# Weight-block sums of a two-level block-product FFN: from instructions on GpSimd to accumulating transfers

## The reference

```
def conv_ffn(hn, w_ffn_in, conv_w, conv_b, w_ffn_down):
    u, v = jnp.split(hn @ w_ffn_in, 2, axis=-1)          # 1024 -> 2 x 2816
    uc = conv_b
    for t in range(CONV_W):                               # width 3
        uc = uc + up[:, t:t + L] * conv_w[t]
    return (jax.nn.gelu(uc) * v).astype(dt) @ w_ffn_down  # 2816 -> 1024
```

## Time and profile before

| | us |
|---|---|
| median of 3 runs | 1282.95 (1281.03 to 1283.58) |
| the profiled execution | 1282.7 |
| its span, first to last instruction | 1280.9 |
| TensorE busy | 1219.8 (95%) |
| VectorE busy | 875.3 (68%) |
| ACT busy | 528.7 (41%) |
| GpSimd busy | 195.6 (15%) |

### The profile page before, as it was taken

One profiled execution on the slowest core, in us unless ns is written; L12 is line 12 of the kernel. 1 busy time (PEld: TensorE's weight loads), 2 busy tenths in 40 slices (PEclk: granted clock), 3 DMA queues, 4 the chain that ended last, 5 costly groups with the idle time before them and its releaser, 6 DMA issues.

```text
span 1280.9 us, 18435 instructions
## 1 busy us (share of the span) xinstructions
PE 1219.8 (95%) x6989; PEld 1108.8 (87%) x6989; DVE 875.3 (68%) x1189; ACT 528.7 (41%) x832; POOL 195.6 (15%) x137
## 2 busy tenths in 40 slices
PE   6999999999999999999999979899899899899977
PEld 5999999999999988888888869789789789789965
DVE  7494585486377372232233799988998998898987
ACT  5353353335245152122221456535535535535544
POOL 0000000000000000000000314324324333433340
PEclk9999999999999999999999999999899899899989
DMA  4311111101201011111123012112121121121302
GB/s 168 134 35 49 68 44 50 61 33 49 78 33 49 34 54 62 66 62 69 65 94 131 22 66 80 53 68 81 50 77 72 50 83 66 50 82 67 115 17 99
DMA packets 23185, 86.14 MB, mean 67 GB/s; under 512 B 2512, under 2 KB 2768, under 8 KB 23120
## 3 DMA queue, kind: packets, MB, share of 16 engines
q1 hardware_dynamic: 22544, 83.90, 17.7%
q10 hardware_dynamic: 576, 1.38, 0.3%
HBM read 82.12 MB, written 3.15 MB: 67 GB/s over the span
## 4 chain that ended last, share of the span: by engine, by line
PE 83%; DVE 10%; issue 2%; DVEq 2%; ACT 1%; DMA 1%; POOL 0%; SPq 0%; ACTq 0%; POOLq 0%
PE ps L1507 43%; PE ps L1750 19%; PE ps L1833 10%; PE ps L1604 3%; PE ps L1544 3%; DVE ring L1232 2%; PE ps L1597 1%; PE ps L1614 1%; PE ps L1532 1%; DVE cb L1315 1%; DVE cb L1296 1%; DVEq L1301 1%; DVE af L1251 1%; PE ps L1534 1%; DVE h L1219 1%
## 5 line engine op out<-in xcount | busy, mean ns | idle before, releaser
L1507 PE MATMUL ps<-hn,ring 128*128 128x256 f32 (+1 forms) x2544 | 462.6, 337 | 0.3 <-DVE hn L921 0.3
L1507 PEld LDWEIGHTS ps<-hn,ring 128*128 128x128 f32 x2544 | 388.3, 191 | 46.7 <-issue 0.7
L1750 PE MATMUL ps<-af,ring 128*128 128x384 f32 x1848 | 334.0, 340 | 33.0 <-DVE v L1288 21.0
L1750 PEld LDWEIGHTS ps<-af,ring 128*128 128x128 f32 x1848 | 325.8, 191 | 40.3 <-DVE v L1288 22.3
L1833 PE MATMUL ps<-ring,gf 128*128 128x512 f32 x693 | 161.0, 394 | 7.1 <-DVE gf L1331 6.8
L892 DVE TENSOR_TENSOR ring<-raw,ring 128x1024 fp32r<-128x1024 f32 x68 | 83.1, 1224 | 119.2 <-ACT ring L476 114.8
L1833 PEld LDWEIGHTS ps<-ring,gf 128*128 128x128 f32 x693 | 132.0, 191 | 35.1 <-issue 7.8
L1232 DVE TENSOR_TENSOR ring<-raw,ring 128x512 fp32r<-128x512 f32 x164 | 127.5, 810 | 13.5 <-ACT ring L713 13.3
L713 ACT ACTIVATE ring<-raw 128x512 fp32r<-128x512 f32 x164 | 96.6, 621 | 53.2 <-DMA raw<-in_pairs 42.0
L1467 POOL TENSOR_TENSOR sums<-raw 128x512 f32<-128x512 f32 x1 | 1.3, 1283 | 707.0 <-DMA raw<-in_pairs 707.0
L525 ACT ACTIVATE sig<-ps 128x768 f32<-128x768 f32 x36 | 29.2, 812 | 179.9 <-PE ps L1507 179.9
(11 more groups left out here) (171 smaller groups left out, 1297.8 us busy)
## 6 DMA issues: line engine op xcount, KB each, us to landing
raw<-in_units SPq DMA_DIRECT2D x68, 512.0 KB, 3.4
raw<-in_pairs SPq DMA_DIRECT2D x66, 512.0 KB, 3.5
strips<-in_strips SPq DMA_DIRECT2D x4, 896.0 KB, 4.6
x_in<-in_x_s SPq DMA_DIRECT2D x4, 512.0 KB, 5.4
h<-in_x_s SPq DMA_DIRECT2D x1, 2048.0 KB, 8.0
y_s<-hw SPq DMA_DIRECT2D x4, 512.0 KB, 3.0
x_in<-in_x_p SPq DMA_DIRECT2D x2, 512.0 KB, 7.4
h<-in_x_p SPq DMA_DIRECT2D x1, 1024.0 KB, 10.4
```

Of the source, the lines that this page charges most:

```text
L1507: ins = pe.matmul(out, w if stationary_w else x, x if stationary_w else w, start=start and i == 0, stop=stop and i == 2)
L1750: ins = pe.matmul(ps[:, bank, 0:HALF], ring[:, p, a, k * P:(k + 1) * P], af[:, x, b, k, :], start=first and k == 0 and j == 0, stop=k == H ...
```

## The change

All sums of weight blocks become additions, so that a transfer can make them: S1 = b11+b12, S3 = b12+b22, S2 = b11+b12+b22, A22 = S2+b21. The token forms, joins, gate sums and residuals change their signs to suit (S2's and S3's results are subtracted from the residual).

- The sums of pairs 1 and on are made by transfers that add a block from HBM to what lies in SBUF (`accum_op=ALU.add`). GpSimd issues them, in the order S2, S3, S1, A22. S2 has three addends: SP loads b11 a second time from HBM into the pair's "second" buffer, a transfer adds b12, GpSimd waits for its semaphore `half_sum`, and another adds b22. So S2 doesn't wait for S1. A22 adds b21 to S2, once S2 is split.
- SP's first load of a pair now waits for A12 and S1 of the buffer's pair before, the new 256 KB load for its A22, the second load for its S3 and S4. Pair 0's sums stay instructions on GpSimd; pair 1's three leave VectorE.
- Order on VectorE: the four gate sums are a function of their own, `gate_sums`, which comes behind `join_third` of the next pair. At a stage's end `conv`, `gate` and `gate_lo` of its last pair each come one down form later. In the last stage `gate_lo(20)` comes ahead of the convolution, and two forms of pair 21 ahead of the gate sums. ACT's gelu moves to suit.
- At the start of the feed-forward part TensorE takes S1 of pair 0 ahead of its S2, and VectorE and ACT make the token forms in that order.

```diff
+        def sum_weights(pool, j, x):
+            b = raw_of(j)
+            r, second = raws[b], seconds[b]
+            u, v = pairs[j, 0], pairs[j, 1]
+            if x == S3:
+                pool.wait_ge(pv_ld[b], 16 * loads_of(j))
+                out, block = r[:, 1, 0:PIECE], v[:, PIECE:UNIT]
             elif x == S2:
+                pool.wait_ge(sec_ld[b], 16 * sums_of(j))
+                pool.dma_start(second, v[:, 0:PIECE], accum_op=ALU.add).then_inc(half_sum[b], 16)
+                pool.wait_ge(half_sum[b], 16 * sums_of(j))
+                out, block = second, v[:, PIECE:UNIT]
+            elif x == S1:
+                pool.wait_ge(pu_ld[b], 16 * loads_of(j))
+                pool.wait_ge(flo, ORD[j, A11] + 1)
+                out, block = r[:, 0, 0:PIECE], v[:, 0:PIECE]
             else:
+                pool.wait_ge(flo, ORD[j, S2] + 1)
+                out, block = second, u[:, PIECE:UNIT]
+            pool.dma_start(out, block, accum_op=ALU.add).then_inc(t_sum[x][b], 16)
...
                 else:
-                    sp.wait_ge(flo, ORD[prior, A22] + 1)
+                    sp.wait_ge(flo, max(ORD[prior, A12], ORD[prior, S1]) + 1)
                 sp.dma_start(raws[b][:, 0, :], pairs[j, 0]).then_inc(pu_ld[b], 16)
+                if j > 0:
+                    if prior is not None:
+                        sp.wait_ge(flo, ORD[prior, A22] + 1)
+                    sp.dma_start(seconds[b], pairs[j, 0][:, 0:PIECE]).then_inc(sec_ld[b], 16)
                 if prior is not None:
-                    sp.wait_ge(flo, ORD[prior, S4] + 1)
+                    sp.wait_ge(flo, max(ORD[prior, S3], ORD[prior, S4]) + 1)
                 sp.dma_start(raws[b][:, 1, :], pairs[j, 1]).then_inc(pv_ld[b], 16)
...
                     if i > 0:
                         join_third(i)
+                    if i > lo and i % 2 == 0:
+                        gate_sums(i - 1)
                     if i > lo and i < NF - 1:
                         gate_lo(i - 1)
                 lo_upto(PLACE[hi - 1, A22] + 5)
                 lo_upto(PLACE[hi - 1, S4] + 5)
                 join_last(hi - 1)
-                conv(hi - 1)
                 if hi == NF:
+                    gate_lo(NF - 2)
+                    conv(hi - 1)
                     gate(NF - 1)
-                    gate_lo(NF - 1)
+                    gate_lo(NF - 1, GATES[1:3])
+                    gate_sums(NF - 1)
+                    gate_lo(NF - 1, GATES[3:])
                 for n, x in enumerate(DOWN[d]):
...
                         if n == 0:
+                            conv(hi - 1)
+                        elif n == 1:
                             gate(hi - 1)
-                        elif n == 1:
+                        elif n == 2:
                             gate_lo(hi - 1)
...
             pool.wait_ge(y_done, NT + 2)
             for x in SUMS:
                 combine_tokens(pool, 0, x, s_done, 0)
 
-            pool.wait_ge(t_done, DIFF[1, S3])
-            for j, x in DIFFS[7:]:
-                difference(pool, j, x)
+            for j, x in SUMMED[4:]:
+                sum_weights(pool, j, x)
```

More of the change, by code:

```diff
@@ L78, in taken @@
         if i == 0:
-            out += [(0, A11), (0, A12), (1, A11), (1, A12), (0, S2), (0, S1), (0, S3)]
+            out += [(0, A11), (0, A12), (1, A11), (1, A12), (0, S1), (0, S2), (0, S3)]
             continue
@@ L111 @@
     SEQ += list(range(_lo, _hi)) + [down_pair(_q) for _q in _qs]
-    DIFFS += [(_i, _x) for _i in range(_lo, _hi) for _x in (S1, S2, S3, A22)]
-    DIFFS += [(down_pair(_q), _x) for _xs in ((S1, S2), (S3,), (A22,)) for _q in _qs for _x in _xs]
-DIFF = {_f: _n + 1 for _n, _f in enumerate(DIFFS)}
+    SUMMED += [(_i, _x) for _i in range(_lo, _hi) for _x in (S2, S3, S1, A22)]
+    SUMMED += [(down_pair(_q), _x) for _xs in ((S2, S3), (S1,), (A22,)) for _q in _qs for _x in _xs]
 LAST_Q = NQ - 1
@@ L124, in loads_of, with sums_of @@
     return sum(raw_of(i) == raw_of(j) for i in SEQ[:SEQ.index(j) + 1])
+def sums_of(j):
+    return sum(i > 0 and raw_of(i) == raw_of(j) for i in SEQ[:SEQ.index(j) + 1])
 def prior_of(j):
@@ L283, in build @@
         pv_ld = [sem(f"pair_v_loaded{b}") for b in range(3)]
-        fhi, flo, fdone, t_done = sem("piece_hi"), sem("piece_lo"), sem("product_done"), sem("weights_combined")
+        fhi, flo, fdone, first_sum = sem("piece_hi"), sem("piece_lo"), sem("product_done"), sem("first_weights_combined")
+        sec_ld = [sem(f"second_loaded{b}") for b in range(3)]
+        half_sum = [sem(f"half_summed{b}") for b in range(3)]
+        t_sum = {x: [sem(f"weights{x}_summed{b}") for b in range(3)] for x in (S1, S2, S3, A22)}
         s_done, s_last, fyhi, fylo = sem("tokens_combined"), sem("last_tokens_combined"), sem("forms_hi"), sem("forms_lo")
@@ L375, in form_source @@
             a11, a12, a21, a22, second = token_blocks(t - 3)
-            return {S3: a11, S4: a12, S1: a21, A22: a22, S2: second}[x]
+            return {S2: a11, S4: a12, S3: a21, A22: a22, S1: second}[x]
         def form_place(o, x, b):
@@ L857, in _ @@
                     if n == 1 and hi < NF:
+                        gelu(hi - 1)
+                    if n == 2 and hi < NF:
                         gate_hi(hi - 1)
@@ L1215, in _, with residual @@
                     dve.drain()
-            def residual(t, half, bank):
+            def residual(t, half, bank, minus=False):
                 hs = h[:, t, 512 * half:512 * half + 512]
+                if minus:
+                    return dve.tensor_tensor(hs, hs, ps[:, bank, :], ALU.subtract).then_inc(h_up, 1)
                 return dve.tensor_tensor(hs, ps[:, bank, :], hs, ALU.add).then_inc(h_up, 1)
@@ L1318, in gate, with gate_lo @@
                 dve.wait_ge(gs_done, 4 * q + 1)
-                dve.tensor_tensor(GATE[S2], GATE[A22], GATE[S3], ALU.subtract).then_inc(gs_done, 1)
-                dve.tensor_tensor(GATE[S1], ge[:, HALF:T], GATE[A22], ALU.add).then_inc(gs_done, 1)
-                if i == NF - 1:
-                    gate_lo(i - 1)
+                dve.tensor_tensor(GATE[S1], ge[:, HALF:T], GATE[A22], ALU.subtract).then_inc(gs_done, 1)
                 dve.wait_ge(gs_done, 4 * q + 2)
+                dve.tensor_tensor(GATE[S2], GATE[S1], ge[:, 0:HALF], ALU.subtract).then_inc(gs_done, 1)
+                dve.wait_ge(gs_done, 4 * q + 3)
                 dve.wait_ge(g_lo, gate_form(q, A11))
-                dve.tensor_tensor(GATE[S4], GATE[A12], GATE[S2], ALU.subtract).then_inc(gs_done, 1)
-            def gate_lo(i):
+                dve.tensor_tensor(GATE[S4], GATE[A12], GATE[S2], ALU.add).then_inc(gs_done, 1)
+            def gate_lo(i, forms=None):
                 q = i // 2
-                for x in GATES[:1] if i % 2 == 0 else GATES[1:]:
+                for x in forms or (GATES[:1] if i % 2 == 0 else GATES[1:]):
                     dve.wait_ge(g_hi, gate_form(q, x))
@@ L1795, in ffn @@
                     if i == 0:
+                        pe.wait_ge(fylo, FORMS.index((5, S1)) + 1)
+                        product(0, S1, BANK_C, True)
                         pe.wait_ge(fylo, FORMS.index((5, S2)) + 1)
@@ L1800, in ffn @@
                         pe.wait_ge(c12_dn, i)
-                    else:
-                        pe.wait_ge(fylo, FORMS.index((5, S1)) + 1)
-                    product(i, S1, BANK_C, True)
+                        product(i, S1, BANK_C, True)
                     if i == 0:
```

104 lines of the change are left out of this document (44 added, 60 removed).

## The result

| | before | after |
|---|---|---|
| median, us | 1283.0 (1281.0 to 1283.6) | 1313.0 (1310.6 to 1315.3) |
| span of the profiled execution, us | 1280.9 | 1308.8 |
| ratio after / before | | 1.0236, 95% interval 1.0215 to 1.0258 |

The change makes the kernel 2.4% slower. The forecast was 1261 with a range from 1243 to 1286.

What follows compares the result with a forecast made beforehand. The prediction took TensorE, busy in 95% of the span, as the bound, with gains only in its gaps. It summed 1282.7-28.8-8-1-0.3+17 = 1261.6 and said 1261 us, range 1243 to 1286.

Steps and rivals of the forecast that it cites:

- The bound and the removal: Four stage ends: TensorE loses time only in gaps; its waits for `join_third` go, -28.8 us.
- (b): Four stage ends: `join_third` ahead of the gate sums; claimed enough alone to remove TensorE's wait of 5.2 us each.
- The last stage: Last stage's down products: gate low half ahead of the convolution, about -8 us; sixth down piece 1.2 us late.
- The place and the mechanism of the new stall: Start of stages 1 to 4: buffer freed late, then load and two additions; TensorE waits 3.0 us, four times.
- L: Time of one summing transfer from issue to semaphore; taken as 4.5 us, lower bound 3.5, upper 6.5 or so.
- 2L-6: New TensorE stall at each start of stages 1 to 4, from two additions in a row: 3.0 us.
- Hidden and free: Extra 256 KB load and about 1.3 MB of sums per pair: no cost, against engines moving 67 to 80 GB/s.
- it costs 0.3 us at L = 4.5: ACT at the start of stages 1 to 4: A22's sum delays `first_copy(lo)` by 0.3 us each.
- The clock: Slow matmuls behind the new stall at the start of stages 1 to 4: 1.0 us each.
- Stage 0's start: Start of (1, S1): VectorE sheds three sums of 0.7 us, but A22's split waits for a transfer; about -1 us.
- The chain of transfers decides: Rival, first pair of stages 1 to 4: load and two sums, then A22's; 36 us or more cancels the gain; chance 0.2.
- GpSimd still slows VectorE: Rival: GpSimd's descriptor preparation stretches VectorE instructions, about 4 x 4 us over the forecast, 1277; chance 0.08.

Runs made afterwards that it cites:

- The order alone: The changed kernel with all weight-block sums as GpSimd instructions again, without the extra load, SP's first load waiting for A22 as before: 1280.67 us, ratio 0.9986.
- the other second buffer: The changed kernel, but the first pair of stages 1 to 4 makes S2 and A22 in the gate sums' space: 1276.24 us, ratio 0.9955.

## Why the prediction was wrong

- **The bound and the removal: right.** The four stage-end waits went, with short forms on VectorE (0.95 and 0.55 us) as forecast, and each stage end lost 7.2 us on average. But "The wait is gone, with (b) alone" is half the truth. The order alone takes that wait away and gives most of it back among the down products, 11.9 us and 4.8 us: 1280.67. The transfers carry that gain, by freeing VectorE.
- **The last stage: right.** -6.5 instead of -8; the sixth down piece is 1.59 us late, 1.2 was forecast.
- **The place and the mechanism of the new stall: right**, confirmed by the other second buffer. TensorE waits for `h` at the start of stages 1 to 4, VectorE for ACT, ACT for a transfer into `tb`.
- **The step that failed first: the length L of a sum in "2L-6".** The stall is a small difference of long terms, and nearly all were a little short: buffer free +0.7, load +0.8 (3.6 for 2.8), the two additions +1.4 (6.4 and 4.0 for 4.5 each), tail +0.2. That makes 3.0 into 6.2 us in stage 1, and 6.2 to 8.0 in the four, where the first additions took 6.4 to 7.6 us. The cause is in the sentence "Hidden and free: the extra load ... and about 1.3 MB of sums per pair". I priced bytes against the bandwidth in use, and not what they do to the transfer that TensorE waits for. The experiment that holds the other loads back gives 3.1 us of each stall to that company. With little beside it an addition takes 4.0 to 4.4 us, and L = 4.5 was a fair value.
- **The second failed step: "it costs 0.3 us at L = 4.5", and "most sums have room for L".** I looked at A22's sum alone. S3's and S1's sums, 6.8 us in the median, stand on GpSimd behind the wait for the half sum. `third_copy` stands behind them on ACT: 0.8, 1.3, 2.0 and 2.6 us behind the four starts, 13.3 us in all. The diff told it, in one line: a wait in the queue that issues all sums. I named what was behind that wait as "only sums that are needed later" and did not ask when. The half sum issued early takes 9 us off these waits and 12 off the time. The 3.8 us for `second_copy` stand on ACT too, behind a transfer into `raw`; I had no term for them, and no run tests them.
- **The clock: 1.0 us taken, 1.6 to 2.6 us measured** behind each start, and 3.0 behind the wait of 4.20 us in stage 0. Each new wait brings its slow matmuls: in all TensorE's busy time is some 15 us above the forecast's, almost a third of the miss, and only 5 of that stand right behind the four waits that I had priced.
- **Stage 0's start: -1 forecast, +3.2 measured.** I had named the transfer for (1, A22) as the risk and priced it below the three sums shed. It takes 6.4 us from issue to use.
- **The rivals.** "The chain of transfers decides" was the true one. Its price of 36 us at L = 5.8 and 52 at L = 7 fits L in company: 10.4 us for both additions and 0.8 more for the load are worth L of 5.6. Yet for that it gives about 1280 (1282.7-38.1+36), since it too left out the queue on GpSimd and the full cost of the clock. "GpSimd still slows VectorE" fell: a gate multiplication takes 0.95 us beside transfers.
- **The chances.** 0.79 for faster leaned on a guess of L that no row bore, with a break-even at L = 5.8 that lay only 1.3 us above it. A multiplied term (four places, two sums each) deserved more weight on its upper end.

## What to carry to other kernels

An operation moved from an engine to a queue that other transfers share must be priced in company: first what else that queue carries at the moment in question, then what waits in the issuing engine's own order behind a semaphore. A reordering that only moves work past a late instruction gives the stall back at the next deadline if the work remains long; a change that shortens it keeps the gain. Where an engine's contention hurts only in some stretches, move only those stretches' work: transfers for the 11 down pairs and most of pair 1 gained 2.0%, transfers for all of pairs 1 and on lost 2.4%.

## What the runs showed of the hardware

- An accumulating transfer of 256 KB takes 4.0 to 4.4 us with little beside it, 4.8 in the median and 6.8 behind others. The page "DMA: Bandwidth & Descriptors" of the Trainium skill (Anatomy of one DMA) gives 2.6 us by estimate for a GpSimd transfer of that size; no run here shows so short a one, and the measurement decides.
- Such transfers hold the DMA engines 2.1 times as long per byte as the loads (in part by their smaller packets), here and in the kernel with transfers for the down pairs (18.5% for 15.73 MB against 22.7% for 40.38 MB).
- Its issue keeps GpSimd for 0.9 us, and VectorE's instructions beside it are not stretched.
- The clock fell behind a wait of 2.93 us (25 matmuls in 6.09 us, granted clock 0.50) and stayed up behind one of 1.53 us (granted clock 1.00). Between them the wait's length alone did not decide: it stayed up behind 2.12 us in the kernel before, and fell behind 2.17 us where pair 1 has instructions (12 matmuls in 3.82 us, 2.4 at full clock).
